# Two expert layers on one core: gathered activations for 64 instead of 32 tokens, a narrower product with U, and half a block of the routing matrix kept in SBUF

## The chip, the cores and the metric

One Trainium2 chip, one of its NeuronCores. The metric is the device time of one execution in microseconds (us); three timed runs give a median. A profile of one execution gives every instruction's start and length on each engine: TensorE (PE; PEld is its weight load), VectorE (DVE), ScalarE (ACT), GpSimd (POOL), and the queues that issue transfers (SP).

## The reference

The program computes a small decoder trunk for 512 tokens of width 1024: layer 0 mixes with an RWKV-7 recurrence, layer 1 with causal pooling, and each is followed by an expert layer ("PEER") with 16384 experts. The expert layers take most of the time, and the change is in them alone:

```
def peer_ffn(h, w_q, keys, u_tab, v_tab):          # 8 heads, 128 keys, top 16
    q = (h @ w_q).reshape(B, S, 8, 2, 128)
    s = einsum('bshpd,hpkd->bshpk', q, keys)
    s_top, i_top = top_k(s, 16)
    cand = s_top[..., 0, :, None] + s_top[..., 1, None, :]      # 16 x 16 candidates
    best, pos = top_k(cand, 16)
    idx = ...                                                   # one of 128 * 128 experts
    gate = softmax(best)
    act = gelu(einsum('thkd,td->thk', u_tab[idx], h))           # exact gelu
    return einsum('thk,thkd->td', gate * act, v_tab[idx])
```

Every token so uses 8 x 16 = 128 of 16384 rows of U and of V. All is float32 and the output must agree with the reference in it.

## The kernel before

`phase_peer` handles one expert layer. The 512 tokens are four blocks of 128. Block 3 is done by gathering: GpSimd fetches for slot s (128 of them) one row of U per token by an indirect transfer (`fetch_u`), VectorE multiplies it by the tokens' activations and sums over the row (`dot`, L2380), and in the V stage it adds 128 gathered rows of V times their weights (`add_row`, L2391).

Blocks 0 to 2 (384 tokens) are done densely. The experts are cut in ET = 128 tiles of 128. For each tile `u_product` (L2069) multiplies all 128 rows of U with the tokens' h: 8 slices of the width, three products each (a number is split into a rounded high part and a low part: high x high, high x low, low x high), so 24 matmuls, each with its own weight load. Their moving operand is UD = 352 tokens wide and not 384: the activations of the last OWN = 32 tokens of block 2 are taken from gathered rows of U too. They need 128 slots each, and since 32 tokens fill a quarter of the partitions, COPIES = 4 copies of them take a quarter of the slots each: 32 more dots, 160 in a layer. ScalarE applies gelu to the product (L2158), and SP stores it to DRAM (`gelu_dram`). ScalarE also rounds the tile of U that comes three tiles later (`uhi`, L2162), and GpSimd subtracts to get its low part (`low_u`, L2319); six tiles of U are in flight.

The order of work is written out by hand, per engine, over the 128 tiles:

- Heads, tiles 0 to 55. Each head takes seven tiles. At its first one TensorE computes the queries (48 matmuls of 512 columns) and the scores; ScalarE copies the scores out; VectorE finds the top 16 of either half (`top16`), adds them to candidates (L2427), finds the top 16 of these, and turns positions into expert numbers with one-hot products (L2447 to L2453). Between the steps `fill` puts one dot at a time, if `may_dot` allows it; `together` has twelve such places in a head, and HEAD_DOTS = 10 are used from head 2 on. GpSimd fetches up to AT_ONCE = 2 rows a tile into eight buffers, as far as `dots_by` says, and waits until the buffer's dot is done.
- Between, tiles 56 to 65. ScalarE takes the exponential once all heads are done (L2255, at tile 62), VectorE normalises the weights, TensorE transposes slots to tokens (`slotT`), and the first one-hots are made. The dots of the own tokens that are left (BETWEEN_DOTS = 8) stand here, four ahead of the first pair of one-hots, four behind the first groups.
- Blocks, tiles 66 to 113. Each tile has two groups of four tokens. For a group VectorE compares numbers with the tokens' indices (`pair`, L2479), ScalarE multiplies three of four one-hots by their weights (`gate_group`, L2204) and VectorE makes the fourth (L2484); TensorE multiplies one-hot by gated one-hot (`spread_group`, L2079), which gives a token's 128 x 128 routing matrix; ScalarE copies it to `wb` (L2195), which holds two half blocks of 64 tokens; SP stores each half in four pieces of 1 MB to DRAM (`store_piece`). The weights of the 32 own tokens are multiplied by their activations first, so their activation counts as 1 later.
- Tail, tiles 114 to 127: the gathered rows of V begin, and the first tiles of V are loaded.

Then the V stage, again 128 tiles: SP loads a tile of V, two tiles' share of the routing matrix (`wt`, six half blocks) and the stored activations (`gl`, 352 wide, with 1.0 behind them). VectorE multiplies matrix by activations (`weigh`, L2508), ScalarE rounds the product (`take_p`, L2217), VectorE makes its low part (`low_p`, L2512); ScalarE and GpSimd split V the same way; TensorE adds 18 matmuls of 512 columns into PSUM (`v_tile`, L2113).

The transfers of SP and GpSimd run on the same 16 DMA engines.

## Time and profile before

| | us |
|---|---|
| median of three timed runs | 3166.78 |
| lowest, highest | 3166.71, 3169.4 |
| span of the profiled execution | 3168.2 |
| its stages in layer 0: product with U begins, V stage begins, V stage ends | 598, 1276, 1802 |
| TensorE busy | 3080.1 (97%) |
| VectorE busy | 2642.7 (83%) |
| GpSimd busy | 2111.8 (67%) |
| ScalarE busy | 1338.7 (42%) |
| bytes moved | 883.09 MB, mean 279 GB/s |

The span is counted from the first to the last instruction; no time around it is given for the profiled execution. A busy share is the time in which at least one instruction of the engine was running, and an instruction that is held up after it began counts as running. In a table by stage, the numbers behind the stretch are, for PE, PEld, DVE, ACT and POOL, the busy time with the count of instructions, then the granted clock of TensorE (1.00 is the higher level), the busy share of the DMA engines and GB/s. A timeline row gives start, length, engine, line, operation, output and inputs with their shapes; "x8" means that so many in a row were merged, and brackets behind it give idle time before it with what ended it.

### The profile page before, as it was taken

What the parts mean: (1) busy time and instruction counts of PE and PEld (TensorE: products, weight loads), DVE (VectorE), ACT (ScalarE), POOL (GpSimd) and SP (SyncE); (2) the same over time, 40 slices, a digit from 0 to 9 for tenths busy, and PEclk for the clock granted to TensorE, in tenths of its full rate; (3) what the DMA queues carried; (4) which work ended last, traced back from release to release, by engine and by line L of the source; (5) the groups of instructions that cost most, each with busy time, mean ns of one, the idle gap of its engine ahead of it and who ended that gap; (6) DMA issues with size and microseconds to landing.
All of it is one profiled execution on the core that took longest, in us unless ns stands there. A gap on an engine that the chain in (4) does not pass through costs nothing. (4 is left out here: it accounts for less than half of the span.)

```text
span 3168.2 us, 57859 instructions
## 1 busy us (share of the span) xinstructions
PE 3080.1 (97%) x21401; PEld 2643.9 (83%) x21401; DVE 2642.7 (83%) x4447; ACT 1338.7 (42%) x2400; POOL 2111.8 (67%) x1366
## 2 busy tenths in 40 slices
PE   8999998999999999999999899999999999999998
PEld 3437887799999999888888677999999998888886
DVE  8875664689999995999999656799989958999997
ACT  0125453333346775333333423333367753333333
POOL 1213444478877777888888604788777778888884
PEclk9999999999999999999999999999999999999999
DMA  9950002588878999999999614788789999999995
GB/s 341 328 200 24 4 5 100 167 289 285 274 242 322 389 389 370 371 350 351 366 350 349 208 57 158 275 286 275 237 318 384 396 369 376 348 350 366 351 349 177
DMA packets 379378, 883.09 MB, mean 279 GB/s; under 512 B 39513, under 2 KB 208017, under 8 KB 370962
## 3 DMA queue, kind: packets, MB, share of 16 engines
q1 hardware_dynamic: 284690, 536.14, 47.8%
q0 software_dynamic: 94464, 343.97, 30.0%
q8 instruction: 139, 2.28, 0.3%
q14 instruction: 85, 0.70, 0.1%
HBM read 780.21 MB, written 98.62 MB: 277 GB/s over the span
## 5 line engine op out<-in xcount | busy, mean ns | idle before, releaser
L2069 PE MATMUL peer_acc<-peer_hhi,peer_uhi 128*128 128x352 f32 x2048 | 673.2, 329 | 1.1 <-POOL peer0same_ulo L2319 0.5
L2069 PE MATMUL peer_acc<-peer_hlo,peer_uhi 128*128 128x352 f32 x2048 | 662.4, 323 | 0.0
L2380 DVE SCALAR_TENSOR_TENSOR peer_row<-peer_row,peer_acc 128x1024 f32<-128x1024 f32 x320 | 385.6, 1206 | 19.7 <-DMA peer_row<-in_pe_u,peer_idx 14.0
L2319 POOL TENSOR_TENSOR peer1same_ulo<-ahead_u,peer_uhi 128x1024 fp32r<-128x1024 f32 x128 | 308.7, 2413 | 127.3 <-ACT peer_uhi L2162 124.0
L2319 POOL TENSOR_TENSOR peer0same_ulo<-ahead_u,peer_uhi 128x1024 fp32r<-128x1024 f32 x128 | 309.6, 2420 | 125.8 <-ACT peer_uhi L2162 121.6
L2069 PEld LDWEIGHTS peer_acc<-peer_hhi,peer_uhi 128*128 128x128 f32 x2048 | 387.9, 189 | 2.7 <-POOL peer0same_ulo L2319 0.8
L2069 PEld LDWEIGHTS peer_acc<-peer_hlo,peer_uhi 128*128 128x128 f32 x2048 | 386.7, 189 | 1.0 <-issue 0.5
L2348 POOL TENSOR_TENSOR peer1lsame_vlo<-peer1l_v,peer1l_vhi 128x1024 fp32r<-128x1024 f32 x128 | 308.6, 2411 | 68.1 <-ACT peer1l_vhi L2211 67.6
L2348 POOL TENSOR_TENSOR peer0lsame_vlo<-peer0l_v,peer0l_vhi 128x1024 fp32r<-128x1024 f32 x128 | 308.4, 2410 | 67.9 <-ACT peer0l_vhi L2211 67.4
L2391 DVE SCALAR_TENSOR_TENSOR peer_acc<-peer_row,peer_p_g,peer_acc 128x1024 f32<-128x1024 f32 x254 | 325.1, 1280 | 20.1 <-DMA peer_row<-in_pe_v,peer_idx 19.6
L2069 PE MATMUL peer_acc<-peer_hhi,peer0same_ulo 128*128 128x352 f32 x1024 | 331.7, 324 | 0.0
L2069 PE MATMUL peer_acc<-peer_hhi,peer1same_ulo 128*128 128x352 f32 x1024 | 331.3, 324 | 0.0
L2113 PE MATMUL peer_acc<-peer0l_vhi,peer0l_phi 128*128 128x512 f32 x768 | 299.4, 390 | 3.3 <-DVE peer0l_plo L2512 1.8
L2296 POOL DMA_INDIRECT peer_row<-in_pe_v,peer_idx x256 | 276.7, 1081 | 38.6 <-issue 8.3
L2113 PE MATMUL peer_acc<-peer1l_vhi,peer1l_phi 128*128 128x512 f32 x768 | 299.2, 390 | 3.1 <-DVE peer1l_plo L2512 1.8
L2113 PE MATMUL peer_acc<-peer1lsame_vlo,peer1l_phi 128*128 128x512 f32 x768 | 298.8, 389 | 0.0
L2113 PE MATMUL peer_acc<-peer0l_vhi,peer0l_plo 128*128 128x512 f32 x768 | 298.8, 389 | 0.0
L2113 PE MATMUL peer_acc<-peer1l_vhi,peer1l_plo 128*128 128x512 f32 x768 | 298.8, 389 | 0.0
L2113 PE MATMUL peer_acc<-peer0lsame_vlo,peer0l_phi 128*128 128x512 f32 x768 | 298.8, 389 | 0.0
L2296 POOL DMA_INDIRECT peer_row<-in_pe_u,peer_idx x256 | 246.8, 964 | 57.3 <-issue 50.5
L2158 ACT ACTIVATE peer_gel<-peer_acc 128x352 f32<-128x352 f32 x256 | 118.1, 461 | 380.0 <-PE peer_acc L2069 350.8
L2162 ACT ACTIVATE peer_uhi<-ahead_u 128x1024 fp32r<-128x1024 f32 x250 | 262.6, 1050 | 2.8 <-DMA ahead_u<-in_pe_uT 2.8
(516 smaller groups left out, 7094.1 us busy)
## 6 DMA issues: line engine op xcount, KB each, us to landing
ahead_u<-in_pe_uT SPq DMA_DIRECT2D x256, 512.0 KB
peer0l_v<-in_pe_v SPq DMA_DIRECT2D x128, 512.0 KB
peer1l_v<-in_pe_v SPq DMA_DIRECT2D x128, 512.0 KB
activations<-peer_gel SPq DMA_DIRECT2D x256, 176.0 KB
rw_g<-in_ada POOLq DMA_DIRECT2D x60, 512.0 KB
routing<-peer0m_wb SPq DMA_DIRECT2D x24, 1024.0 KB
peer0l_wt<-routing SPq DMA_DIRECT2D x64, 384.0 KB
routing<-peer1m_wb SPq DMA_DIRECT2D x24, 1024.0 KB
```

Source lines behind the costliest of these rows:

```text
L2069: mm = pe.matmul(ub[e % 2][:, 0:UD], a, h[:, k, 0:UD], start=(n == 0), stop=(n == 3 * KT - 1))
L2113: mm = pe.matmul(acc[:, t, ds], a[:, ts], w[:, ds], start=(begin and n == 0), stop=(end and n == 2), skip_group_check=True)
L2158: a.activation(gel[:, e % NL], ub[e % 2][:, 0:UD], ACT.Gelu).then_inc(gel_made, 1)
L2162: a.activation(uhi[:, n % NH], u[:, n % NU], ACT.Copy).then_inc(uhi_made, 1)
L2296: g.indirect_dma_start(row[:, at % NG], None, table, bass.IndirectOffsetOnAxis(ap=of, axis=0)).then_inc(row_loaded[at % NG], 16)
L2319: g.tensor_tensor(ulo[:, q].rearrange("p k e -> p (k e)"), u[:, q].rearrange("p k e -> p (k e)"), uhi[:, e % NH].bitcast(F32).rearrange("p ...
L2348: g.tensor_tensor(vlo[:, q], vr[:, q], vhi[:, e % NH].bitcast(F32), ALU.subtract).then_inc(vlo_made, 1)
L2380: v.scalar_tensor_tensor(out=row[:, m % NG], in0=row[:, m % NG], scalar=1.0, in1=h_own if mine else h_g, op0=ALU.mult, op1=ALU.mult, accum ...
L2391: v.scalar_tensor_tensor(out=acc_g, in0=row[:, at % NG], scalar=p_g[:, s:s + 1], in1=acc_g, op0=ALU.mult, op1=ALU.add).then_inc(acc_made, 1)
```

## The change

Twice as many tokens of block 2 (OWN = 64, half the block) get their activations from gathered rows of U. UD is 320, and so is the width of the products with U, of gelu and of the stored activations. COPIES is 2, so the own slots are 64 and the dots 192 in a layer: 12 a head from head 2 on, 16 between (eight ahead of the first one-hots, eight behind the first groups), 96 later. GpSimd may fetch three rows a tile (four once) instead of two. ScalarE gates all four one-hots of a group, and VectorE makes none.

The own tokens are now a whole half block. Since their routing weights carry their activations already, this half isn't stored: it stays in `wb[:, 1]`, five half blocks (STORED) go to DRAM and come back, `weigh` multiplies 320 columns, and `take_p` and `low_p` handle the 64 own columns by an instruction of their own. To make room, rounded V takes the place of rounded U, the activations of the V stage lie in `kept` rows, `phi` lies over `slotT` and `plo` over the last tile of U. The memset of 1.0 and the wait for the second half's store before it go. ScalarE's loop over the V tiles is written out.

```diff
@@ -1731 @@
-H_AT, U_AT, MIXER_H_AT = 82688, 40192, 78336
+H_AT, U_AT, MIXER_H_AT = 82432, 40448, 78336
...
-OWN = 32
-COPIES = 4
+OWN = 64
+COPIES = 2
...
-HEAD_DOTS = 10
-BETWEEN_DOTS = 8
+HEAD_DOTS = 12
+BETWEEN_DOTS = 16
...
-ACT_GATES = 3
+U_AT_ONCE, LAST_AT_ONCE = 3, 4
...
-EXP_AT, TURN_AT, OWN_BY = 4, 3, 6
+EXP_AT, TURN_AT, OWN_BY = 4, 3, 10
@@ -1782 @@
+        STORED = 2 * DT - 1
+        assert OWN == P // 2
...
+        assert HEAD_DOTS == 3 * HEAD_OWN // 2
@@ -1800 @@
-                return AT_DOTS - BETWEEN_DOTS + max(0, min(e - AT_BETWEEN - HEAD_OWN, HEAD_OWN))
+                return AT_DOTS - BETWEEN_DOTS + max(0, min(2 * (e - AT_BETWEEN - 4), HEAD_OWN))
@@ -1813 @@
-                half, r = divmod(i, HEAD_DOTS // 2)
-                if r in (1, 3):
-                    return True, HEAD_OWN * q + 2 * half + r // 2
-                return False, FIRST_DOTS + q * (HEAD_DOTS - HEAD_OWN) + 3 * half + r // 2
+                three, r = divmod(i, 3)
+                if r:
+                    return True, HEAD_OWN * q + 2 * three + r - 1
+                return False, FIRST_DOTS + q * (HEAD_DOTS - HEAD_OWN) + three
@@ -1836 @@
+        phi = Arena(nc, arena.prefix + "p", arena.offset, arena.end)("phi", [P, NH, SD], F32R)
@@ -1851 @@
-        assert ending.offset <= arena.offset + 4 * (NU + NH) * KT * P
+        plo = Arena(nc, arena.prefix + "lo", arena.offset + 4 * NU * KT * P - 4 * NH * SD, arena.end)("plo", [P, NH, SD], F32R)
+        assert ending.offset <= arena.offset + 4 * NU * KT * P - 4 * NH * SD <= arena.offset + 4 * (NU - 1) * KT * P
@@ -1886 @@
-        wt, gl = late("wt", [P, NU // 2, 2 * DT, 2, P // 2]), late("gl", [P, NU, SD])
-        vhi = late("vhi", [P, NH, D], F32R)
-        phi, plo = late("phi", [P, NH, SD], F32R), late("plo", [P, NH, SD], F32R)
-        pf = [kept[n][:, 0:SD] for n in ("gate", "g_row", "b_row")]
-        assert len(pf) == NH
+        wt = late("wt", [P, NU // 2, STORED, 2, P // 2])
+        assert late.offset <= shared + 4 * P * P // 2
+        w_own = wb[:, 1]
+        vhi = [uhi[:, (q + ET) % NH].rearrange("p k e -> p (k e)") for q in range(NH)]
+        pf = [kept[n][:, 0:UD] for n in ("gate", "g_row", "b_row")]
+        gl = [kept[n][:, UD * (1 + q):UD * (2 + q)] for n in ("gate", "g_row", "b_row") for q in range(2)]
+        assert len(pf) == NH and len(gl) == NU and 3 * UD <= D
@@ -1949 @@
-                    t, half = divmod(hh, 2)
+                    half = hh % 2
...
-                    sp.dma_start(w_dram[t, half, :, rows_].rearrange("j i t -> j (i t)"),
+                    sp.dma_start(w_dram[hh, :, rows_].rearrange("j i t -> j (i t)"),
@@ -1959 @@
-                                     w_dram[:, :, :, bass.ds(e, 2)].rearrange("b h j i t -> j (b h) (i t)")).then_inc(wt_loaded[q // 2], 16)
-                    sp.dma_start(gl[:, q, 0:UD], gelu_dram[bass.ds(e, 1)].rearrange("a j t -> (a j) t")).then_inc(gl_loaded[q], 16)
+                                     w_dram[:, :, bass.ds(e, 2)].rearrange("b j i t -> j b (i t)")).then_inc(wt_loaded[q // 2], 16)
+                    sp.dma_start(gl[q], gelu_dram[bass.ds(e, 1)].rearrange("a j t -> (a j) t")).then_inc(gl_loaded[q], 16)
@@ -1994 @@
-                    if 1 <= hh <= 2 * DT and r < PIECES:
+                    if 1 <= hh <= STORED and r < PIECES:
...
-                            sp.wait_ge(w_stored[half], 16 * PIECES * DT)
+                            sp.wait_ge(w_stored[half], 16 * PIECES * ((STORED + 1 - half) // 2))
@@ -2071 @@
-                    pe.wait_ge(gated, ACT_GATES * (n + 1))
-                    pe.wait_ge(i_made, n + 1)
+                    pe.wait_ge(gated, G * (n + 1))
@@ -2108 @@
-                        for n, (a, w) in enumerate(((phi[:, q % NH], vhi[:, q % NH]), (phi[:, q % NH], vlo[:, q % NU]),
-                                                     (plo[:, q % NH], vhi[:, q % NH]))):
+                        for n, (a, w) in enumerate(((phi[:, q % NH], vhi[q % NH]), (phi[:, q % NH], vlo[:, q % NU]),
+                                                     (plo[:, q % NH], vhi[q % NH]))):
@@ -2200 @@
-                    for q in range(ACT_GATES):
+                    for q in range(G):
...
-                def take_v(q, turns, e):
-                    act.wait_ge(v_loaded[q % NU], 16 * (TURN // NU) * turns + 16 * (q // NU) + 16)
-                    if q >= NH:
+                def take_v(e):
+                    act.wait_ge(v_loaded[e % NU], 16 * (e // NU) + 16)
+                    if e >= NH:
...
-                    a.activation(vhi[:, q % NH], vr[:, q % NU], ACT.Copy).then_inc(vhi_made, 1)
-
-                def take_p(q, e):
+                    a.activation(vhi[e % NH], vr[:, e % NU], ACT.Copy).then_inc(vhi_made, 1)
+                def take_p(e):
...
-                    if q >= NH:
+                    if e >= NH:
...
-                    a.activation(phi[:, q % NH], pf[q % NH], ACT.Copy).then_inc(phi_made, 1)
+                    a.activation(phi[:, e % NH, UD:SD], w_own[:, e], ACT.Copy)
+                    a.activation(phi[:, e % NH, 0:UD], pf[e % NH], ACT.Copy).then_inc(phi_made, 1)
@@ -2262 @@
-                        take_v(e - (ET - 2), 0, e - (ET - 2))
-                        take_p(e - (ET - 2), e - (ET - 2))
-                for e in range(2, 4):
-                    take_p(e, e)
-                    take_v(e, 0, e)
-                with act.Fori(0, V_TURNS) as i:
-                    for q in range(TURN):
-                        take_p(4 + q, TURN * i + (4 + q))
-                        take_v(4 + q, i, TURN * i + (4 + q))
-                norm_dev(nc, act, nt, 0, acc_g)
-                for e in range(4 + TURN * V_TURNS, ET):
-                    take_p(e, e)
-                    take_v(e, 0, e)
+                        take_v(e - (ET - 2))
+                        take_p(e - (ET - 2))
+                for e in range(2, ET):
+                    if e == 4 + TURN * V_TURNS:
+                        norm_dev(nc, act, nt, 0, acc_g)
+                    take_p(e)
+                    take_v(e)
@@ -2334 @@
-                    for _ in range(HEAD_OWN if e == AT_BETWEEN + MOVE_LAST + 2 + NH else AT_ONCE):
+                    for _ in range(LAST_AT_ONCE if e == AT_BETWEEN + MOVE_LAST + 2 + NH else U_AT_ONCE):
@@ -2475 @@
-                        dve.wait_ge(gated, ACT_GATES * (n - 1))
+                        dve.wait_ge(gated, G * (n - 1))
...
-                    if n * G == UD:
-                        dve.wait_ge(own_taken, 1)
-                    for q in range(n * G + ACT_GATES, (n + 1) * G):
-                        ins = v.tensor_scalar(hot_i[:, n % 2, q % G], numbers, slotT[:, 1, q:q + 1], slotT[:, 0, q:q + 1], ALU.is_equal,
-                                              ALU.mult)
-                    ins.then_inc(i_made, 1)
@@ -2505 @@
-                    v.tensor_tensor(parts(pf[e % NH]), parts(gl[:, e % NU]), wt[:, e % NU // 2, :, e % 2], ALU.mult).then_inc(pf_made, 1)
+                    v.tensor_tensor(parts(pf[e % NH]), parts(gl[e % NU]), wt[:, e % NU // 2, :, e % 2], ALU.mult).then_inc(pf_made, 1)
...
-                    v.tensor_tensor(plo[:, e % NH], pf[e % NH], phi[:, e % NH].bitcast(F32), ALU.subtract).then_inc(plo_made, 1)
+                    v.tensor_tensor(plo[:, e % NH, 0:UD], pf[e % NH], phi[:, e % NH, 0:UD].bitcast(F32), ALU.subtract)
+                    v.tensor_tensor(plo[:, e % NH, UD:SD], w_own[:, e], phi[:, e % NH, UD:SD].bitcast(F32), ALU.subtract).then_inc(plo_made, 1)
...
-                dve.wait_ge(w_stored[1], 16 * PIECES * DT)
-                ch(v.memset(gl[:, :, UD:SD], 1.0))
```

## Rows read from the trace of the kernel before

**Rows 1.** The page: busy time and share of each engine.

```profile
PE 3080.1 (97%) x21401; PEld 2643.9 (83%) x21401; DVE 2642.7 (83%) x4447; ACT 1338.7 (42%) x2400; POOL 2111.8 (67%) x1366
```

**Rows 2.** Layer 0 by stage: heads 2 to 6, between, blocks, V stage.

```profile
693.00:891.00 198.00, 198.00 (x1162) 188.50 (x1161) 195.61 (x671) 68.79 (x100) 158.55 (x95) 1.00 0.82 280
891.00:985.00 94.00, 91.17 (x589) 90.48 (x588) 87.09 (x189) 50.16 (x98) 70.46 (x40) 0.98 0.77 266
985.00:1224.00 239.00, 239.00 (x1692) 238.60 (x1691) 215.20 (x325) 174.54 (x420) 172.83 (x118) 1.00 0.98 380
1276.00:1802.00 526.00, 523.08 (x2301) 431.51 (x2302) 486.71 (x393) 197.19 (x269) 443.34 (x249) 1.00 0.98 342
```

**Rows 3.** TensorE's timeline, product with U: start us, length us, instruction.

```profile
894.73 0.32 PE L2069 MATMUL peer_acc<-peer_hhi,peer_uhi 128*128 128x352 f32 x1
...
904.81 0.32 PE L2069 MATMUL peer_acc<-peer_hhi,peer_uhi 128*128 128x352 f32 x1
```

**Rows 4.** TensorE's timeline, product with V.

```profile
1499.86 0.39 PE L2113 MATMUL peer_acc<-peer0l_vhi,peer0l_plo 128*128 128x512 f32 x1
...
1504.62 0.39 PE L2113 MATMUL peer_acc<-peer0l_vhi,peer0l_plo 128*128 128x512 f32 x1
```

**Rows 5.** TensorE's timeline in the blocks: eight spread matmuls, then the next tile.

```profile
1100.88 1.05 PE L2079 MATMUL peer_acc<-kept_b_row,kept_gate 128*128 128x128 f32 x8
...
1102.58 0.41 PE L2069 MATMUL peer_acc<-peer_hhi,peer_uhi 128*128 128x352 f32 x1
```

**Rows 6.** VectorE's timeline, head 6, from the last step of head 5.

```profile
848.27 2.35 DVE L2453 TENSOR_SCALAR peer_idx<-peer0a_idx_f 128x32 uint32<-128x32 f32 x1
...
869.02 2.44 DVE L2427 TENSOR_TENSOR kept_b_row<-peer0a_val 128x256 f32<-128x256 f32 x2
...
883.09 2.54 DVE L2447 TENSOR_TENSOR peer0a_hot<-const_made,peer0a_half_f 128x1024 bf16<-128x1024 f32 x1
...
887.88 2.34 DVE L2453 TENSOR_SCALAR peer_idx<-peer0a_idx_f 128x32 uint32<-128x32 f32 x1
```

**Rows 7.** GpSimd's timeline beside it.

```profile
882.15 2.40 POOL L2319 TENSOR_TENSOR peer0same_ulo<-ahead_u,peer_uhi 128x1024 fp32r<-128x1024 f32 x1 [5.35 <-ACT peer_uhi L2162]
...
887.78 2.40 POOL L2319 TENSOR_TENSOR peer0same_ulo<-ahead_u,peer_uhi 128x1024 fp32r<-128x1024 f32 x1
```

**Rows 8.** VectorE's timeline, the same steps in heads 0, 1 and 7.

```profile
615.08 2.34 DVE L2427 TENSOR_TENSOR kept_b_row<-peer0a_val 128x256 f32<-128x256 f32 x2
...
633.25 1.22 DVE L2447 TENSOR_TENSOR peer0a_hot<-const_made,peer0a_half_f 128x1024 bf16<-128x1024 f32 x1
...
636.71 0.18 DVE L2453 TENSOR_SCALAR peer_idx<-peer0a_idx_f 128x32 uint32<-128x32 f32 x1
...
663.78 2.80 DVE L2427 TENSOR_TENSOR kept_b_row<-peer0a_val 128x256 f32<-128x256 f32 x2
...
908.62 5.97 DVE L2427 TENSOR_TENSOR kept_b_row<-peer0a_val 128x256 f32<-128x256 f32 x2
```

**Rows 9.** VectorE's waits, 600 to 1000 us: us, times, longest.

```profile
DVE peer0a_val L2411 <- ACT peer0a_sc L2174: 7.5, 2, 7.3
```

**Rows 10.** The page's groups: a dot, a fetch.

```profile
L2380 DVE SCALAR_TENSOR_TENSOR peer_row<-peer_row,peer_acc 128x1024 f32<-128x1024 f32 x320 | 385.6, 1206 | 19.7 <-DMA peer_row<-in_pe_u,peer_idx 14.0
...
L2296 POOL DMA_INDIRECT peer_row<-in_pe_u,peer_idx x256 | 246.8, 964 | 57.3 <-issue 50.5
```

**Rows 11.** ScalarE's timeline: gates of the second group, the activation behind them.

```profile
946.87 0.99 ACT L2204 ACTIVATE kept_b_row<-kept_g_row,peer_slotT 128x128 f32<-128x128 f32 x3 [0.34 <-issue]
947.76 0.44 ACT L2158 ACTIVATE peer_gel<-peer_acc 128x352 f32<-128x352 f32 x1
```

**Rows 12.** The DMA view of 1070 to 1190 us, in the blocks: 40 slices.

```profile
GB/s 430 404 410 388 365 317 321 281 340 414 416 427 415 430 405 419 422 415 411 411 340 283 348 319 415 422 414 417 424 425 420 404 420 411 396 357 327 322 327 419
DMA packets 13322, 46.36 MB, mean 386 GB/s; under 512 B 1482, under 2 KB 4257, under 8 KB 12039
```

**Rows 13.** VectorE's timeline, the low part in the V stage.

```profile
1504.94 2.50 DVE L2512 TENSOR_TENSOR peer0l_plo<-kept_gate,peer0l_phi 128x384 fp32r<-128x384 f32 x1
```

More of the change, by code:

```diff
@@ L1912, in phase_peer @@
         whi_made, wlo_made, iota_made = sem("whi"), sem("wlo"), sem("iota")
-        j_made, i_made, spread_done, taken = sem("hot_j"), sem("hot_i"), sem("spread"), sem("taken")
+        j_made, spread_done, taken = sem("hots"), sem("spread"), sem("taken")
         w_stored = [sem("w0_stored"), sem("w1_stored")]
@@ L2347, in _ @@
                     pool.wait_ge(vhi_made, e + 1)
-                    g.tensor_tensor(vlo[:, q], vr[:, q], vhi[:, e % NH].bitcast(F32), ALU.subtract).then_inc(vlo_made, 1)
+                    g.tensor_tensor(vlo[:, q], vr[:, q], vhi[e % NH].bitcast(F32), ALU.subtract).then_inc(vlo_made, 1)
                     for _ in range(AT_ONCE):
@@ L2557, in hybrid_trunk @@
     mod_rows = dram("mod_rows", [DEPTH * N_MOD * D])
-    w_dram = dram("routing", [TT - 1, 2, P, P, P // 2])
+    w_dram = dram("routing", [2 * (TT - 1) - 1, P, P, P // 2])
     gelu_dram = dram("activations", [pe_uT.shape[1], P, S - P - OWN])
```

## The prediction

> **What bounds the kernel now.** The page first: TensorE is busy 97% of the span and VectorE 83% [rows 1]. A mean over stages hides who could give way where, so the second view is the table by stage of layer 0 (layer 1 has the same stages). In heads 2 to 6, TensorE is busy 198.00 of 198.00 us, but VectorE is busy 195.61 of them too; in the stretch between, 91 and 87 of 94; in the blocks 239 and 215 of 239; in the V stage 523 and 487 of 526 [rows 2]. So TensorE sets the pace nearly everywhere, and in the heads VectorE stands right behind it.
>
> The third view is TensorE's timeline. In the product with U, 63 matmuls lie between the two rows: 10.08 us / 63 = 0.160 us from start to start at 352 columns [rows 3]. In the product with V it is 4.76 / 21 = 0.2267 us at 512 columns [rows 4]. The recorded lengths (0.32, 0.39) overlap; only the starts give the rate. The difference, 66.7 ns over 160 columns, is 0.417 ns a column, one column per cycle at the higher clock level (2.4 GHz; granted clock 1.00 in rows 2), with 13 ns on top of both. 32 columns fewer are then 13.3 ns a matmul, 24 x 13.3 = 0.32 us a tile.
>
> The fourth view is VectorE's timeline of one head. From L2453 of head 5 (848.27) to L2453 of head 6 (887.88) are 39.61 us [rows 6], and VectorE waited for scores only twice in the layer, at the start of heads 0 and 1 by the times and the longest of 7.3 us [rows 9]. So in heads 2 to 7 it runs late behind TensorE and its gaps are not idle time but lengthened instructions: L2453 makes 32 numbers in 2.34 us at 887.88, but in 0.18 us in head 0 [rows 6, 8], and GpSimd had begun a subtraction of 2.40 us at 887.78 [rows 7]. It ended when that ended. These waits are in VectorE's "busy" time.
>
> **The change, part by part**, against the profiled execution's span of 3168.2 us (the page gives nothing around it; the timed runs are 3166.7 to 3169.4, median 3166.8, and I apply the difference to the median).
>
> *Narrower products.* 128 tiles x 0.32 = 41 us a layer, 82 us in all, if TensorE sets every tile.
>
> *32 more dots a layer.* A dot is 1.21 us, some 0.07 overlapping with the next instruction, so 1.14 [rows 10]. 12 fall to heads 2 to 7 (2 each, 12 instead of 10), 4 more stand between the weights and the first pair of one-hots (8 instead of 4), 16 in the blocks or their first groups.
>
> *Heads.* TensorE would want 39.61 - 7 x 0.32 = 37.4 us a head. VectorE's own need is 39.61 less its waits: L2453 2.34 - 0.18 = 2.2; L2447 2.54 - 1.22 = 1.3; L2427, two instructions, 2.44 less some 0.75 (an estimate: 448 results at L2447's rate and 0.1 each) = 1.7; together 5.2, so 34.4 [rows 6, 8]. With two dots 36.7. That leaves 0.7 us for waits in a head of 37.4. Until now TensorE's pace fixed at which phase GpSimd's subtractions meet VectorE, and the waits only filled what was free. Where nothing fixes it: in head 0 L2427 waits 1.6 and the others nothing; in head 1 L2427 waits 2.05, in head 7 it alone 5.2 [rows 8]. Bounds for the waits of a head are 0.7 (TensorE stays the bound) and 8; I take 5.3, the value of the locked heads, between head 0 and head 7. The head is then 42.0 us, 2.4 longer than now, and VectorE is the bound. Five such heads: +12. Head 7 has long waits already: 0 (its two dots against a more usual wait). Head 2 starts earlier, since head 1's scores come 2.2 us sooner and three fetches a tile shorten its wait for rows: -4 (bounds 0 and -7). GpSimd gets two fetches of 0.96 more a head [rows 10] on 158.55 busy of 198 [rows 2]: 31.7 + 1.9 of 37.4, with gaps of some tenths after each; it fits, but with nothing to spare.
>
> The Trainium skill's page "SBUF — State Buffer" (section "Who interferes with whom") says that a VectorE instruction with two SBUF inputs, or in a two-port mode, shares a lock with GpSimd and blocks for its whole instruction. The trace agrees at 887.78 to 890.2. By that rule a late VectorE meets a new subtraction each time, and the waits don't vanish by being late; if it were wrong the sum would be that of rival A.
>
> *Between.* ScalarE waits at the gates for VectorE, and its activation of the next tile comes right behind them (946.87 + 0.99, then 947.76) [rows 11]; TensorE needs that activation. So VectorE's chain is the path here: 4 dots +4.6, a fourth gate in ScalarE for each of two groups +0.6, two one-hots of VectorE gone -0.5: +4.7. TensorE, ahead by what it saved, waits.
>
> *Blocks and tail.* From tile 67 on TensorE is the bound: 61 x 0.32 = -19.5. Per tile there are two groups, together 1.70 us of spread matmuls (1100.88 to 1102.58) [rows 5]; they don't change. VectorE loses 96 one-hots and gets 12 dots, so it has cover (215 of 239 busy). ScalarE gets two gates a tile, 0.33 each by the 0.99 for three: 174.5/239 of 5.64 is 4.1, now 4.8 of 5.32 [rows 2, 11]. Some groups get two dots, and the odd one-hot behind them comes over a microsecond later: ten times 0.2, +2. The queues: now a tile moves 512 KB of U, 176 of activations, 1.75 rows of 512, and 512 of the matrix, 2.15 MB in 5.64 us = 381 GB/s, as measured (386) [rows 12]. Then 512 + 160 + 1024 + 512 KB = 2.26 MB in 5.32 = 425 GB/s, while a half is being stored. The best slices show 425 to 430, most full ones 410 to 420 [rows 12]. The six tiles of U in flight take up most; +1 (bounds 0 and +15, where the gain of 48 tiles is gone).
>
> The same skill's "DMA: Bandwidth & Descriptors" (section "Specifications") gives an HBM limit of about 358 GB/s a core. The trace passes it, at a mean of 386, so it is not used.
>
> *V stage.* TensorE keeps 18 x 0.2267 us a tile. The low part is cut in two and the rounding too. VectorE's low part lies at 2.50 us because GpSimd's subtraction holds it [rows 13]; its own need is some 0.4 and the second piece some 0.1. All is made about a tile ahead, so 0 (bounds -2 and +4 a layer). The smaller loads, the memset, the wait that it stood behind and the last half's store: 0.
>
> Sum for a layer: -4 + 12 + 0 + 4.7 - 19.5 + 2 + 1 = -3.8, for two -7.6: **3159 us**. One microsecond of waits more or less in a head moves it by 12 (six heads, two layers).
>
> **The rivals.**
>
> A. The waits stay within what is free and TensorE is the bound in the heads. Then 66 tiles give -21, with +4.7 and the blocks' -16.5: -33 a layer, 3101. For it: they do fit exactly now. Against: three places where VectorE meets GpSimd, 0.7 us for all. With waits of 2.5 us, halfway, it is 3159 - 34 = 3125.
>
> B. Slower: with VectorE late by more, its last steps in a head, which now begin in the gap that the query leaves GpSimd (5.35 us idle ahead of 882.15) [rows 7], come to lie among dense subtractions, two of them back to back. 5.2 us at L2427 in head 7 is such a case [rows 8]. With 8 us a head, 3159 + 32 = 3191. It is slower from waits of about 6 us on. For it: head 7; against: head 0 and the heads as they are.
>
> C. The queues set the blocks: at 400 GB/s a tile takes 5.65 us, nothing is gained in 48 tiles: +15.4 less 1 a layer, 3159 + 29 = 3188. For it: full slices at 410 to 420. Against: dips to 281 to 320 in between, where less was asked for [rows 12].
>
> D. The 0.160 us is a floor (of loading weights) and not columns: no tile is faster, and the heads and the between lose the same, since VectorE sets them: 3159 + 39 = 3198. Against: the difference to 512 columns is exactly one cycle a column, and the spread matmuls, with a load before each, start every 0.11 us (1.70 / 16) [rows 5].
>
> **How the numbers follow.** Forecast (waits 4.3 to 6.3 a head, 3147 to 3171) 0.40; halfway to A 0.20; A 0.08; B 0.20; C 0.07; D 0.05. A difference under 0.2%, 6 us, can't be told from none here, so faster is under 3160.5, slower over 3173.1. Of the forecast's 0.40, 0.24 is faster and 0.15 within; halfway and A are faster, 0.28; of the rest 0.02 each goes to faster and within. Faster 0.54, same 0.17, slower 0.29. The range of 8 in 10 reaches from halfway's far side to B: 3112 to 3190; the likeliest case's own is 3147 to 3171.
>
> **What would show it.** Starts of the U matmuls 0.1467 us apart (D: 0.160). L2453 to L2453 in heads 2 to 6: 42.0 us (A: 37.4, B: 45), TensorE no longer 198 of 198 there, and waits of GpSimd's fetches for dots or of ScalarE for VectorE. Between: several microseconds of idle TensorE, and its granted clock down there. Blocks: 5.32 us a tile (C: 5.6). V tiles: 4.08 us. The forecast is wrong if VectorE's head is under 40 us or over 44.

## The result and the profile after

The changed kernel takes 3237.41 us (median of four runs, 3236.63 to 3238.73) against 3166.77 (3166.71 to 3169.4): a ratio of 1.022, 95% interval 1.0208 to 1.0233. It is slower by 70.6 us, where 3159 was forecast in a range that ended at 3190.

The page after, busy time and then two of its groups. Each group row ends with the idle time of the engine just before the instructions and what ended most of it.

```profile
PE 3041.8 (94%) x21401; PEld 2588.8 (80%) x21401; DVE 2671.3 (83%) x4637; ACT 1413.9 (44%) x2848; POOL 2173.7 (67%) x1430
...
L2381 DVE SCALAR_TENSOR_TENSOR peer_row<-peer_row,peer_acc 128x1024 f32<-128x1024 f32 x384 | 462.8, 1209 | 91.1 <-DMA peer_row<-in_pe_u,peer_idx 84.7
...
L2297 POOL DMA_INDIRECT peer_row<-in_pe_u,peer_idx x256 | 257.1, 1004 | 59.7 <-issue 51.2
```

TensorE was given less to do but fell from 97% to 94% busy [rows 1]. A dot costs what it cost (1209 ns for 1206), but VectorE now idles 84.7 us ahead of its dots for a row that has not arrived, where it was 14.0 [rows 10].

The table by stage of layer 0, with the columns of rows 2: heads 2 to 6, between, blocks, V stage.

```profile
691.00:893.00 202.00, 189.63 (x1138) 178.13 (x1137) 200.01 (x660) 66.58 (x97) 167.66 (x104) 0.97 0.86 289
893.00:967.00 74.00, 64.72 (x428) 62.83 (x426) 69.21 (x172) 32.05 (x56) 62.01 (x38) 0.98 0.86 299
967.00:1261.00 294.00, 262.82 (x1876) 256.77 (x1875) 233.39 (x296) 221.20 (x559) 209.97 (x144) 0.98 0.94 358
1310.00:1830.00 520.00, 517.54 (x2281) 427.45 (x2280) 486.60 (x510) 203.06 (x385) 430.53 (x247) 1.00 0.96 333
```

TensorE, 198 of 198 in the heads and 239 of 239 in the blocks before [rows 2], is short by 12 and 31 us now. The row of the blocks in rows 2 leaves out their first 28 us. The whole blocks of the kernel before, to set beside the row of 967 to 1261 above, are:

```profile
957.00:1225.00 268.00, 266.73 (x1874) 266.14 (x1875) 240.15 (x358) 194.40 (x468) 193.31 (x130) 0.99 0.96 365
```

To give each stage its length in both kernels I take the start of ScalarE's activation behind a tile's product with U. These rows are the blocks' borders, tile 67 and tile 114 of layer 0, in the kernel before and then after:

```profile
957.36 0.44 ACT L2158 ACTIVATE peer_gel<-peer_acc 128x352 f32<-128x352 f32 x1
...
1225.34 0.46 ACT L2158 ACTIVATE peer_gel<-peer_acc 128x352 f32<-128x352 f32 x1 [3.27 <-PE peer_acc L2069]
```

```profile
967.07 0.41 ACT L2164 ACTIVATE peer_gel<-peer_acc 128x320 f32<-128x320 f32 x1
...
1261.29 0.44 ACT L2164 ACTIVATE peer_gel<-peer_acc 128x320 f32<-128x320 f32 x1 [2.63 <-PE peer_acc L2076]
```

All stages by such starts, us, layer 0 / layer 1 ("forecast" is the prediction's sum for the same tiles):

| tiles | before | after | difference | forecast |
|---|---|---|---|---|
| ahead of layer 0's first | 602.6 | 600.0 | -2.6 | 0 |
| 0 to 56, heads | 306.7 / 306.7 | 315.6 / 316.1 | +8.9 / +9.4 | +8 |
| 56 to 67, between | 48.0 / 47.7 | 51.4 / 51.4 | +3.4 / +3.7 | +4.7 |
| 67 to 114, blocks | 268.0 / 269.3 | 294.2 / 294.2 | **+26.2 / +24.9** | **-12** |
| 114 to 127, tail | 50.3 / 50.3 | 45.8 / 45.8 | -4.5 / -4.5 | -4.2 |
| last tile to the next layer or the end | 678.4 / 540.2 | 678.4 / 541.8 | 0 / +1.6 | -0.3 |

The differences add up to 66.5 of the spans' 66.6 (3234.8 less 3168.2). The blocks alone missed their forecast by 38 and 37 us, the whole by 74 to 78: the blocks are the miss. Of layer 0's 38 us, 31 are TensorE standing still. It was also busy for 262.8 us where 47 tiles at 5.32 are 250; the mean granted clock of 0.98 accounts for some 6 of these 13 (an estimate, 2% of 294). What held the blocks shows in the waits of the kernel after, 967 to 1261 us (us in total, times, longest):

```profile
ACT kept_b_row L2210 <- DVE kept_g_row L2480: 44.4, 34, 4.5
DVE peer_row L2381 <- DMA peer_row<-in_pe_u,peer_idx: 36.6, 35, 2.5
PEld peer_acc L2085 <- ACT kept_b_row L2210: 36.3, 26, 3.8
PE peer_acc L2085 <- ACT kept_b_row L2210: 30.8, 22, 3.7
```

Read from below: TensorE lost 30.8 us at the spread matmuls, waiting for ScalarE's gates; ScalarE waited for VectorE's one-hots (L2480); and VectorE stood 36.6 us at dots ahead of them. In the kernel before (957 to 1225 us) ScalarE's wait for the one-hots was even longer and cost TensorE almost nothing; the waits that grew are TensorE's, and VectorE's for rows, one of 0.6 us:

```profile
ACT kept_b_row L2204 <- DVE kept_g_row L2479: 67.5, 45, 4.1
PE peer_acc L2079 <- ACT kept_b_row L2204: 2.7, 2, 2.0
DVE peer_row L2380 <- DMA peer_row<-in_pe_u,peer_idx: 0.6, 1, 0.6
```

One such event on VectorE's timeline, then the fetch on GpSimd's, and ScalarE's and TensorE's rows at the same time:

```profile
1149.21 1.21 DVE L2381 SCALAR_TENSOR_TENSOR peer_row<-peer_row,peer_acc 128x1024 f32<-128x1024 f32 x1
...
1171.49 1.22 DVE L2381 SCALAR_TENSOR_TENSOR peer_row<-peer_row,peer_acc 128x1024 f32<-128x1024 f32 x1 [2.23 <-DMA peer_row<-in_pe_u,peer_idx]
1172.64 0.08 DVE L2381 DVE_READ_ACCUMULATOR peer_row<-peer_row,peer_acc 128x1 f32 x1
1172.64 1.22 DVE L2480 TENSOR_TENSOR kept_g_row<-peer_acc,peer_slotT 128x1024 f32<-128x1024 f32 x1
```

```profile
1162.25 0.94 POOL L2297 DMA_INDIRECT peer_row<-in_pe_u,peer_idx  x1 [0.30 <-issue]
```

```profile
1173.89 1.28 ACT L2210 ACTIVATE kept_b_row<-kept_g_row,peer_slotT 128x128 f32<-128x128 f32 x4 [2.94 <-DVE kept_g_row L2480]
```

```profile
1175.22 1.16 PE L2085 MATMUL peer_acc<-kept_b_row,kept_g_row 128*128 128x128 f32 x8 [1.92 <-ACT kept_b_row L2210]
```

The dot at 1149.21 is the eighth before the one at 1171.49, so it is the one that frees that row's buffer. GpSimd asks for the new row at 1162.25, 11.8 us after the dot's end, since it asks by a count of dots three tiles back (FETCH_LAG); the dot begins 9.2 us later, when the row has landed. Dot, lag and landing together are 22.3 us. That is the length of a ring, and it holds for each of the NG = 8 buffers. GpSimd has no wait for a dot in this stretch; it waits 56.6 us for ScalarE's rounding of U (L2168), which keeps it in step with the tiles. So the lag is one of tiles and not of dots.

The means, from the fetches and the landings in the trace (in the blocks, over all dots that the ring serves there, 84 before and 96 after): the ask comes 11.1 us after the dot's end before and 12.2 after, 1.95 tiles in both, and the row has landed 8.3 us after its fetch began in both. The transfer did not become slower on the mean. The 35 rows that a dot waited for were later than that: asked after 12.6 us, landed 9.05 after.

### The profile page after: what moved, and what is told of

Its sections match the earlier page's. It is cut to its first block and busy times, and to the rows that moved or that the text cites. A ratio compares the mean times of both kernels' runs of the same rounds, so it can differ in the third digit from the quotient of the medians.

```text
span 3234.8 us, 58229 instructions
## 1 busy us (share of the span) xinstructions
PE 3041.8 (94%) x21401; PEld 2588.8 (80%) x21401; DVE 2671.3 (83%) x4637; ACT 1413.9 (44%) x2848; POOL 2173.7 (67%) x1430
## 5 line engine op out<-in xcount | busy, mean ns | idle before, releaser
L2076 PE MATMUL peer_acc<-peer_hhi,peer_uhi 128*128 128x320 f32 x2048 | 657.1, 321 | 42.0 <-POOL peer0same_ulo L2320 22.1
L2076 PE MATMUL peer_acc<-peer_hlo,peer_uhi 128*128 128x320 f32 x2048 | 642.4, 314 | 0.0
L2381 DVE SCALAR_TENSOR_TENSOR peer_row<-peer_row,peer_acc 128x1024 f32<-128x1024 f32 x384 | 462.8, 1209 | 91.1 <-DMA peer_row<-in_pe_u,peer_idx 84.7
L2349 POOL TENSOR_TENSOR peer1lsame_vlo<-peer1l_v,peer_uhi 128x1024 fp32r<-128x1024 f32 x128 | 308.6, 2411 | 76.3 <-ACT peer_uhi L2217 75.7
L2349 POOL TENSOR_TENSOR peer0lsame_vlo<-peer0l_v,peer_uhi 128x1024 fp32r<-128x1024 f32 x128 | 308.4, 2409 | 75.2 <-ACT peer_uhi L2217 74.1
L2076 PE MATMUL peer_acc<-peer_hhi,peer1same_ulo 128*128 128x320 f32 x1024 | 321.5, 314 | 0.0
L2076 PE MATMUL peer_acc<-peer_hhi,peer0same_ulo 128*128 128x320 f32 x1024 | 320.0, 312 | 0.0
L2119 PE MATMUL peer_acc<-peer_uhi,peer1p_phi 128*128 128x512 f32 x768 | 299.4, 390 | 4.3 <-DVE peer1lo_plo L2508 2.8
L2119 PE MATMUL peer_acc<-peer_uhi,peer0p_phi 128*128 128x512 f32 x768 | 299.2, 390 | 3.7 <-DVE peer0lo_plo L2508 2.3
L2119 PE MATMUL peer_acc<-peer_uhi,peer1lo_plo 128*128 128x512 f32 x768 | 298.8, 389 | 0.0
L2119 PE MATMUL peer_acc<-peer1lsame_vlo,peer1p_phi 128*128 128x512 f32 x768 | 298.8, 389 | 0.0
L2297 POOL DMA_INDIRECT peer_row<-in_pe_v,peer_idx x256 | 261.2, 1020 | 38.9 <-issue 9.3
L2168 ACT ACTIVATE peer_uhi<-ahead_u 128x1024 fp32r<-128x1024 f32 x250 | 262.1, 1048 | 0.0
```

The source lines that it names most:

```text
L2076: mm = pe.matmul(ub[e % 2][:, 0:UD], a, h[:, k, 0:UD], start=(n == 0), stop=(n == 3 * KT - 1))
L2119: mm = pe.matmul(acc[:, t, ds], a[:, ts], w[:, ds], start=(begin and n == 0), stop=(end and n == 2), skip_group_check=True)
L2168: a.activation(uhi[:, n % NH], u[:, n % NU], ACT.Copy).then_inc(uhi_made, 1)
L2297: g.indirect_dma_start(row[:, at % NG], None, table, bass.IndirectOffsetOnAxis(ap=of, axis=0)).then_inc(row_loaded[at % NG], 16)
L2349: g.tensor_tensor(vlo[:, q], vr[:, q], vhi[e % NH].bitcast(F32), ALU.subtract).then_inc(vlo_made, 1)
L2381: v.scalar_tensor_tensor(out=row[:, m % NG], in0=row[:, m % NG], scalar=1.0, in1=h_own if mine else h_g, op0=ALU.mult, op1=ALU.mult, accum ...
```

## The experiments

**The theories.** R: the ring of row buffers sets the blocks. With n dots a tile it serves NG / n tiles: before, 8 / (84 dots / 45 tiles = 1.87) = 4.3 tiles of 5.70 = 24.4 us, against a round of 1.2 + 11.1 + 8.3 = 20.6. After, 8 / (96 / 43 = 2.23) = 3.6 tiles, at the forecast 5.32 only 19.1 us, against 1.2 + 1.95 x 5.32 + 8.3 = 19.9. So rows are late and the tile stretches, and with it the lag, which is counted in tiles; at the measured 294.2 / 47 = 6.26 the ring has 22.4 us, the 22.3 of the event above. Means alone would let it settle at 5.8 us a tile (3.58 tiles = 1.2 + 1.95 tiles + 8.3), the late rows' 12.6 and 9.05 at 6.5; the measured tile lies between. (The recorded expectations count landing from the end of the fetch, 7.5 us, and leave out the fetch's own 0.95.) Q (rival C of the prediction): the DMA queues are full. S: ScalarE's fourth gate a group sets the blocks. For the heads, P (V in one expectation): VectorE's own work and its waits for GpSimd; G: GpSimd's own order. Where "one run" stands behind a time it is a single one; the four of the kernel after lie 2 us apart.

**One tile less between dot and ask, in the blocks.**

```
+BLOCK_LAG = 2
...
-if e >= FETCH_LAG and n_u < min(NG + dots_by(e - FETCH_LAG), ready_by(e)):
+lag = BLOCK_LAG if e >= AT_IOTA else FETCH_LAG
+if e >= lag and n_u < min(NG + dots_by(e - lag), ready_by(e)):
```

> In the blocks GpSimd may fetch a row of U one tile earlier (a lag of 2 instead of 3 tiles behind the dots that free the buffer); nothing else differs from the changed kernel. There the tiles 67 to 114 took 294.2 us a layer (268.0 before), and 48 tiles at TensorE's pace would be 253. Theory R (the ring of eight rows): 96 dots in 43 tiles use up eight buffers in 3.6 tiles, 19.1 us at TensorE's pace, and a row needs 12.3 us until it is asked for and 7.5 to land, so VectorE waits at the dot, the one-hots behind it are late and TensorE waits for the gates. Asked for one tile (5.3 us) earlier the rows are in time: blocks 255 to 265 us, time 3165 to 3185. Theory S (ScalarE's eight gates a tile make its chain too long): no change, 294. Theory Q (the DMA queues are full): no change or a little, over 285.

3199.24 us, one run, 38 less than after. Blocks 277.7 / 272.4 for 294.2; all other stages as in the kernel after, to 2 us. The row waits of layer 0's blocks are nearly gone (967 to 1245 us, same columns), but one new wait stands there: ScalarE's activation of the own half's dots waits for their move.

```profile
ACT peer_idx L2253 <- DMA peer_idx<-peer_dots_own: 10.4, 1, 10.4
...
DVE peer_row L2383 <- DMA peer_row<-in_pe_u,peer_idx: 3.5, 4, 1.8
```

The bytes are the same and the blocks are 17 to 22 us shorter: for R, and against Q, which allowed nothing under 285. But R had expected 255 to 265 and 3165 to 3185, and both were missed. In layer 0 the one wait of 10.4 us is most of the rest; what else holds the blocks the run does not show.

**Twelve of the 96 dots from the blocks to the tail.**

```
+TAIL_DOTS = 12
...
-return AT_DOTS + IN_BLOCKS * (e - AT_IOTA) // (AT_LAST - AT_IOTA)
-return DOTS
+return AT_DOTS + (IN_BLOCKS - TAIL_DOTS) * (e - AT_IOTA) // (AT_LAST - AT_IOTA)
+return min(DOTS, DOTS - TAIL_DOTS + 4 * (e - AT_LAST + 1))
...
-DOTS_END = 3
+DOTS_END = 6
...
```

> 12 of the 96 dots of the blocks are moved behind them, into the tail, where VectorE is idle three quarters of the time. Rows a tile fall from 2.23 to 1.95 (before: 1.87). Theory R: eight buffers last 4.1 tiles, 21.8 us, against a round trip of 19.8: blocks 255 to 270 us, time 3170 to 3195, with up to 2 us given back in the tail. Theory S: no change in the blocks. Theory Q: bytes a tile in flight fall by 6%, blocks 294 to about 277.

3185.24 us, one run. Blocks 262.7 / 264.0, tail 50.7 / 51.7: 31 us won and 5 to 6 given back. Row waits in the blocks of layer 0 (967 to 1228 us) are 13.0 us for 36.6. Blocks and time came as R expected, and shorter than the 277 that Q gave for 6% fewer bytes. The tail gave back more than the 2 us expected: GpSimd's last fetches of U stand ahead of a remainder of U there, and TensorE waits for it once. Behind the wait it runs at its lower clock level, a granted clock of 0.54 from 1248.5 to 1252.0, with 0.267 us from start to start for 0.1465:

```profile
1248.53 0.42 PE L2077 MATMUL peer_acc<-peer_hhi,peer_uhi 128*128 128x320 f32 x1 [3.16 <-POOL peer0same_ulo L2321]
```

3.2 us of wait and 14 matmuls at 0.12 more are the 4.9 of layer 0.

**Three gates of a group on ScalarE, one on VectorE, as before.**

```
+ACT_GATES = 3
...
-for q in range(G):                  # ScalarE
+for q in range(ACT_GATES):
...
+for q in range(n * G + ACT_GATES, (n + 1) * G):   # VectorE
+    ins = v.tensor_scalar(hot_i[:, n % 2, q % G], numbers, slotT[:, 1, q:q + 1], slotT[:, 0, q:q + 1], ALU.is_equal, ALU.mult)
```

> The one part of the change in the blocks that moves a one-hot from VectorE to ScalarE is undone: ScalarE gates three of four, VectorE makes the fourth. Theory S: ScalarE's chain is 0.66 us a tile shorter, the tiles fall by 0.5 us or more, blocks under 275, time under 3200. Theory R: the rows are as late as before, VectorE has 0.8 us a tile more to do but waits for rows anyway: blocks 290 to 300, time within 15 us of 3237. Theory Q: the same as R.

3244.11 us, one run; blocks 293.8 / 293.9, between 53.9 / 53.8 for 51.4. ScalarE had 28 us less to do there and nothing came of it:

```profile
967.00:1261.00 294.00, 260.77 (x1863) 255.29 (x1863) 264.18 (x390) 193.46 (x468) 208.79 (x145) 0.98 0.95 359
```

S falls. VectorE took on 31 us (264 for 233) and that cost the blocks nothing either, so neither engine's amount of work is the bound there, as R expected. Q expected the same, so this run does not part R from Q.

**The kernel before with six row buffers in use.**

```
-NG = 8
+NG = 6
...
-row = arena("row", [P, NG, D])
+row = arena("row", [P, 8, D])
```

> The kernel before, with 6 instead of 8 row buffers in use (the array keeps its size), all else as it was. Theory R (in the blocks a row is asked for only after its buffer's dot, and comes back some 18.5 us after that dot; the buffers last NG divided by the dots per tile): 6 / 1.87 = 3.2 tiles of 5.64 us = 18.1 us is then below the round trip, as 8 / 2.23 = 3.6 tiles of 5.32 = 19.1 us nearly is in the kernel after, and the blocks grow from 268 to 285 or more per layer, with VectorE's dot waiting on the row's DMA. If anything the slower tile gives part of it back, so not above 310. Total 3200 to 3250. Rival Q (the after kernel's blocks are slow since its transfers fill the DMA queues: 0.94 busy): with the before kernel's own bytes and fewer rows in flight nothing changes, blocks 268 to 272, total within 10 us of 3167.

3244.56 us (3239.7 to 3248.24, four runs), ratio 1.0238 (1.0221 to 1.0255). The stages around them stay within 1.4 us (the part ahead of layer 0's first product is 3.9 shorter); the blocks go from 268.0 / 269.3 to 302.7 / 306.4. The chain of the kernel after appears in the kernel before, at a lower DMA share (0.90 for 0.96, 323 GB/s for 365). Its row by stage and then its waits, both of 955 to 1257 us:

```profile
955.00:1257.00 302.00, 277.48 (x1874) 271.83 (x1875) 239.36 (x358) 195.15 (x466) 191.69 (x129) 0.98 0.90 323
```

```profile
ACT kept_b_row L2204 <- DVE kept_g_row L2479: 59.2, 35, 5.6
DVE peer_row L2380 <- DMA peer_row<-in_pe_u,peer_idx: 46.6, 30, 4.0
PEld peer_acc L2079 <- ACT kept_b_row L2204: 32.6, 24, 4.8
PE peer_acc L2079 <- ACT kept_b_row L2204: 27.1, 21, 4.6
```

This is the strongest evidence for R: nothing but the ring was changed, and the blocks lose 35 and 37 us with the same waits. The ring has 6 / 1.87 = 3.2 tiles of 6.44, 20.7 us, against 1.2 + 11.6 + 7.0 = 19.9 by means. Q, which expected nothing, falls.

**Both cures of the blocks.** BLOCK_LAG = 2 and TAIL_DOTS = 12 as above, DOTS_END 8, and MOVE_AT 10 instead of 14 for the move that ScalarE waited for in the first experiment.

> After's kernel with both cures of the blocks: rows are asked for two tiles instead of three after their dots in the blocks, and 12 of the 96 dots of the blocks move to the tail (which then waits for dots until its tile 8); the move of the own half's dots stands at tile 10 instead of 14. Theory R: the blocks come to what TensorE and VectorE alone would give, 255 to 258 per layer (forecast in the document: 253), the tail 47 to 48, total 3160 to 3170. Rival Q (queues bound the blocks near 5.6 to 5.7 us a tile): blocks no lower than 263, total 3180 or more.

3177.6 us (3173.55 to 3183.4, ten runs), ratio to before 1.0026 (1.0015 to 1.0036). Blocks 260.7 / 260.4, tail 50.6 / 49.6; heads still 315.8 / 315.6. Layer 0's blocks:

```profile
969.00:1229.00 260.00, 251.93 (x1874) 250.21 (x1874) 223.08 (x278) 218.60 (x558) 202.97 (x138) 0.99 0.98 383
```

Some 60 of the 71 us are back, where R had expected 3160 to 3170 and Q 3180 or more. TensorE is busy 252 of 260, and 252 / 47 = 5.36 a tile is the forecast's 5.32: the floor was right, the way to it was not open. 260.5 is under Q's 263 but above the 255 to 258 that R expected, and the tail cost 4 to 5 us instead of 1 to 2. Row waits are down to 1.0 us, but with the DMA engines at a share of 0.98 a wait stands there that the kernels before and after do not have in their blocks: ScalarE, ahead of its rounding, for a tile of U.

```profile
ACT peer_uhi L2170 <- DMA ahead_u<-in_pe_uT: 6.2, 3, 2.6
```

So whether the queues hold the last few microseconds of the relieved blocks stays open; that they held the 294 does not.

**In the heads: two dots of twelve over 64 columns only.** The kernel leaves out the other 960 columns of them.

```
+wide = 64 if 0 <= q < HEADS - 2 and i in (5, 11) else D
-in0=row[:, m % NG], ... in1=h_own if mine else h_g
+in0=row[:, m % NG, 0:wide], ... in1=(h_own if mine else h_g)[:, 0:wide]
```

> In heads 2 to 7, two of the twelve dots take only 64 of 1024 columns (the output isn't the reference's), so VectorE has the dots' time of the kernel before, while the rows, waits and TensorE's narrower products stay those of the changed one. Heads 2 to 6 took 41.5 to 42.0 us there. Theory V (VectorE's own work plus its waits for GpSimd sets the head): a head falls by 2.1 us to 39.4 to 40, heads and the stretch between lose 10 to 14 us a layer, time 3237 - 20 to 28. Rival G (GpSimd, with three fetches at once ahead of its subtraction, sets the head): within 0.5 us of 42 a head, time within 6 us.

3223.31 us, one run, between what the two theories gave. The same code does two things: in layer 0 heads 3 to 6 are 38.2 us each, less than the 39.4 to 40 of V, in layer 1 they are 41.5 to 41.6, as G had it. (The blocks of layer 0 are 299.9 us for 294.2, which takes back part of the gain.) VectorE's last steps of a head, layer 0 and then layer 1 (L2454 here is L2452 of the kernel after):

```profile
835.93 1.27 DVE L2454 SCALAR_TENSOR_TENSOR peer0a_idx_f<-peer0a_slots 128x32 f32<-128x32 f32 x1
```

```profile
2224.45 4.90 DVE L2454 SCALAR_TENSOR_TENSOR peer1a_idx_f<-peer1a_slots 128x32 f32<-128x32 f32 x1
```

In layer 1 two microseconds less work of VectorE bought 0.4. The rest went into three steps that GpSimd's subtractions lengthen: the additions to candidates (L2428 of the kernel after), the second large one-hot (L2448) and the step above. They take 1.58 + 2.80 + 4.90 = 9.3 us in a head, for 0.76 + 2.07 + 4.91 = 7.7 in the kernel after. So a head is still work plus waits, but the waits are not given: they grew as the work shrank.

**GpSimd's fetches ahead of its query remainder.** In the kernel after the heads of 42 us look like this, VectorE's row, then GpSimd's:

```profile
809.18 4.91 DVE L2452 SCALAR_TENSOR_TENSOR peer0a_idx_f<-peer0a_slots 128x32 f32<-128x32 f32 x1
```

```profile
809.25 2.43 POOL L2320 TENSOR_TENSOR peer0same_ulo<-ahead_u,peer_uhi 128x1024 fp32r<-128x1024 f32 x1
811.62 2.42 POOL L2326 TENSOR_TENSOR peer0aover_wlo<-ahead_wq,peer0aover_whi 128x1024 fp32r<-128x1024 f32 x1
817.00 0.95 POOL L2297 DMA_INDIRECT peer_row<-in_pe_u,peer_idx_own  x1 [2.96 <-DMA peer_idx_own<-peer_idx]
```

VectorE's 32 numbers wait out two subtractions back to back (809.25 to 814.04) and end with the second. They become indices, SyncE moves those, and GpSimd's next fetch waits 2.96 us for them; behind it stands the next remainder of U, for which TensorE waits (11.8 us in four heads). I read this as a loop through four engines, each late because of the one before; no run takes a single link out of it. The edit:

```
 for e in range(ET):
     low_u(e)
-    if 0 <= n < HEADS - 1 and r in (1, 3):
-        low_query(n + 1, r // 2)
     for _ in range(...): ... fetch_u(n_u)
+    if 0 <= n < HEADS - 1 and r in (1, 3):
+        low_query(n + 1, r // 2)
```

> After's kernel with one thing changed: in the heads GpSimd issues its row fetches before it makes the next head's query remainder, so that its two subtractions of the keys' and queries' remainders no longer run back to back. Theory P (a tiny VectorE step cannot start while GpSimd runs one subtraction behind another; the 32-number step before the fetch indices takes 4.9 us for that, and the ring of waits VectorE, SyncE's move, GpSimd's fetch goes round with it): that step falls to 2.4 us or less, a head from 41.9 to 39.5 to 40.0, five to six heads, so 10 to 12 us less per layer; the blocks stay at 294. Total about 3215. Rival G (GpSimd's order is what sets the head, any move of its work makes the remainders of U late): a head stays at 41.9 or grows, total 3237 or more.

3236.08 us (3219.86 to 3253.18, four runs), ratio to before 1.0209 (1.016 to 1.0257). P had expected 3215; against the 3237 of the kernel after no gain shows in a spread of 33 us. Again the layers differ: heads of 42.4 us in layer 0, of 39.5 in layer 1, with the step at 2.5 and at 0.19 us (two instances each, shortest, median, longest in ns):

```profile
L2452 DVE SCALAR_TENSOR_TENSOR peer0a_idx_f<-peer0a_slots x2: 2545/2547/2549, 811.7 to 854.1; 128x32 f32<-128x32 f32 x2
```

```profile
L2452 DVE SCALAR_TENSOR_TENSOR peer1a_idx_f<-peer1a_slots x2: 192/192/192, 2193.8 to 2233.3; 128x32 f32<-128x32 f32 x2
```

P is half right: layer 1 gains 10.8 us as expected, layer 0 loses 4.5. There the waits moved to other steps: L2428 2.53 us for 0.76 in the kernel after, L2448 3.18 for 2.07, and the step itself 2.55 for 4.91, together 0.5 us more, which is what the head grew. The blocks, expected at 294, are 297.9 / 296.9. The four runs lie so far apart, where those of the kernel after lie 2 apart; that the layers fall now into the one rhythm and now into the other would do it, but only one run has a trace. Why is open.

**All three together.**

> The two cures of the blocks together with GpSimd's fetches ahead of its query remainder in the heads. If both effects are independent: the combination's time less 20 to 24 us, so 3140 to 3150, which would be faster than before. If the heads are bound by GpSimd's order, no gain over the combination.

3160.61 us (3150.33 to 3168.91, eight runs), ratio to before 0.9973 (0.9956 to 0.9989): faster than both kernels, by a quarter of a per cent over the one before. The profiled run (3152.95) has heads 304.9 / 304.7, blocks 260.4 / 261.2, tail 49.4 / 49.2. Expected were 20 to 24 us less than with the two cures, and 3140 to 3150. The profiled run is 24.8 us under that of the two cures (3177.72), but the medians are only 17 apart and 3160.61 is outside the range. That some runs fall into the longer heads would do that, but only one of them has a trace. Its stages of heads 2 to 6 and blocks:

```profile
693.00:891.00 198.00, 190.07 (x1168) 178.10 (x1168) 193.98 (x695) 67.97 (x99) 167.51 (x106) 1.00 0.87 302
955.00:1216.00 261.00, 254.06 (x1889) 252.11 (x1888) 221.77 (x282) 219.07 (x560) 203.56 (x139) 0.99 0.99 386
```

## Why the prediction was wrong

- *Narrower products, 0.32 us a tile*: right. In a tile of the kernel after the products with U run 1168.88 to 1172.25 for 23 starts, 0.1465 us each; rival D falls. In the tail the gain is there whole, 4.5 us in 13 tiles.
- *Heads, 42.0 us*: the number is right, 41.9, and so is the sum (+8.9 / +9.4 for +8), in part by luck. 36.7 of its own and 5.3 of waits were forecast, but the 5.3 (its own terms add up to 5.2) was that of heads with another pattern: in head 6 before, L2427, L2447 and L2453 were held up and L2451 took 0.19; now that step (L2452) takes 4.91, with 4.7 of the waits, and the one that was L2453 0.18. And I added waits to work as if they were given, and they are not: with 2 us less work the head stays. In the sum two misses cancel: tiles 0 to 21 of layer 0 are 1.2 us shorter and 21 to 56 are 10.1 longer, for a forecast of -4 and +12. Rival B named two subtractions back to back as the bad case, and they were it, at 42 and not at 45.
- *Between, +4.7*: +3.4 and +3.7. Right in kind.
- *Blocks*: the step that failed is "From tile 67 on TensorE is the bound ... VectorE loses 96 one-hots and gets 12 dots, so it has cover (215 of 239 busy)". That asks how much VectorE has to do, not when its rows come. Dots per tile rose by a fifth (1.87 to 2.23), tiles were to become a fifteenth shorter (5.70 to 5.32), and the number of buffers and the lag in tiles stayed: 24.4 us of ring fell to 19.1, against some 20 that a round takes. TensorE's floor of 47 x 5.32 = 250 was right (252 busy with the ring eased); the 31 us that it stood still, and the longer busy time beside them, were not in the sum.
- *Rival C* gave a time of 3188 for blocks that gain nothing. They lost 25 us, and the queues were not fuller: over the whole blocks the DMA share is 0.94 at 358 GB/s where it was 0.96 at 365. The rows that the prediction counted for this rival (1.75 to 2 a tile) it counted as bytes only, never as buffers.
- *Tail, V stage*: -4.5, and 0 / +1.6. Right.
- *The range*: its slow end (3190) was rival B's alone. Had the ring been counted, by the means of the trace before (8 buffers, 2.23 dots a tile, an ask 1.95 tiles after the dot, 8.3 us to land), tiles of 5.8 us would have made some 3194 of it (an estimate: 47 tiles, two layers): slower, outside the range, and still short of 3237, for a dot waits for the late rows and not for the mean one.

## What to carry to other kernels

Where a schedule fetches into a ring of buffers, its capacity in microseconds is buffers / uses per tile x tile time, and a change that raises uses or shortens tiles eats it from both sides; set it against use + lag to the ask + landing, before asking how busy the engines are. Mean times understate the round, since the late row is the one that is waited for. An engine that is far from busy can still stop the others when it waits at an instruction for data and the urgent work stands behind it in order. And waits that come of two engines meeting cannot be added to an engine's own work as if they were fixed: here they grew when the work shrank, and moved to other steps when one cause was taken out. Time several runs and look at every layer, since the same code may settle in more than one rhythm.

## What the runs showed of the hardware that was not expected

- A VectorE step of 0.19 us took 4.91 when two GpSimd subtractions of 2.4 us ran back to back: it did not get in between them.
- The same instructions locked into heads of 38.2 and of 41.6 us in the two layers of one execution (39.5 and 42.5 in another kernel).
- In the relieved blocks the DMA engines moved 383 to 386 GB/s on the mean at a share of 0.98 to 0.99, and TensorE waited only about 8 of 260 us. Whether the queues set those 8 is not shown.
- A stop of TensorE of 3.2 us cost 4.9: for the 3.5 us behind it the granted clock was 0.54 and matmuls started 0.267 us apart for 0.1465.
